# Mean of k's squares from a high and a low fp32r part, with two more rows of q1 in front of it

## The reference, cut to what matters

```python
k = apply_rope(rms_norm(k, k_norm_g[l]), cos, sin)      # mean of squares over the 64 values of a head
q = apply_rope(rms_norm(q, q_norm_g[l]), cos, sin) * q_scale
attn = sliding_sink_attention(q, k, v, sinks[l])
pool = multiscale_pool(u, w_pool[l], pool_scale[l])
h = h + jnp.concatenate([attn, pool], axis=-1) @ w_out[l]
```

## Time and profile before

| what | value |
|---|---|
| median of 3 runs | 1054.25 us (1054.16 to 1055.2) |
| the profiled execution's own time | 1054.56 us |
| its span | 1052.8 us |
| PE busy | 1036.8 us, 98% of the span, 7896 matmuls |
| DVE busy | 687.1 us, 65% |
| ACT busy | 466.1 us, 44% |
| POOL busy | 103.7 us, 10% |
| chain that ended last, by engine | PE 84%, DVE 9%, ACT 4%, issue 2% |
| granted TensorE clock, mean | 0.998 of full speed |

### The profile page before, as it was taken

The page is one execution under the profiler, slowest core; times in us unless marked ns, Lnnn a source line. Parts: engine busy times, 40 slices in busy tenths (PEclk is TensorE's granted clock), DMA queues, the critical chain, the costliest instruction groups (busy, mean ns, idle before and its releaser), DMA issues.

```text
span 1052.8 us, 18748 instructions
## 1 busy us (share of the span) xinstructions
PE 1036.8 (98%) x7896; PEld 990.2 (94%) x7896; DVE 687.1 (65%) x1023; ACT 466.1 (44%) x710; POOL 103.7 (10%) x108
## 2 busy tenths in 40 slices
PE   8999999999999999999999999999999999999998
PEld 7998999999999999999999889999889998899987
DVE  6768645669945599455547784565797557975452
ACT  6986535333423443223338773453442334423322
POOL 1253000110001100011003510000000000000000
PEclk9999999999999999999999999999999999999999
DMA  7210332231333222322231203232223332232212
GB/s 236 87 53 34 106 96 80 81 100 62 117 95 110 81 81 81 121 81 91 84 107 51 81 4 118 81 110 91 81 81 120 99 103 80 80 121 90 92 60 80
DMA packets 94107, 94.96 MB, mean 90 GB/s; under 512 B 3424, under 2 KB 92856, under 8 KB 94024
## 3 DMA queue, kind: packets, MB, share of 16 engines
q1 hardware_dynamic: 93456, 93.58, 27.9%
q10 hardware_dynamic: 312, 0.18, 0.1%
q0 software_dynamic: 256, 0.01, 0.0%
HBM read 91.65 MB, written 2.10 MB: 89 GB/s over the span
## 4 chain that ended last, share of the span: by engine, by line
PE 84%; DVE 9%; ACT 4%; issue 2%; DMA 0%; DVEq 0%; SPq 0%; ACTq 0%
PE slot L571 65%; PE slot L985 12%; PE slot L789 2%; PE slot L629 1%; ACT sumsq L1256 1%; PE slot L1045 1%; PE slot L849 1%; PE slot L856 1%; DVE ms_work L1657 1%; PE slot L821 1%; DVE w_lo L424 1%; DVE k_dup L1669 1%; DVE nmax L1720 1%; DVE m_op_lo L1930 0%; DVE sink_arg L1725 0%
## 5 line engine op out<-in xcount | busy, mean ns | idle before, releaser
L571 PE MATMUL slot<-x_hi,w_hi 128*128 128x264 f32 (+2 forms) x1516 | 353.7, 300 | 0.0
L571 PE MATMUL slot<-x_lo,w_hi 128*128 128x264 f32 (+2 forms) x1516 | 350.0, 298 | 0.0
L571 PE MATMUL slot<-x_hi,w_lo 128*128 128x264 f32 (+2 forms) x1516 | 349.5, 297 | 0.0
L571 PEld LDWEIGHTS slot<-x_hi,w_hi 128*128 128x128 f32 x1516 | 245.8, 189 | 11.1 <-issue 0.7
L571 PEld LDWEIGHTS slot<-x_lo,w_hi 128*128 128x128 f32 x1516 | 244.7, 189 | 7.3
L571 PEld LDWEIGHTS slot<-x_hi,w_lo 128*128 128x128 f32 x1516 | 244.4, 189 | 7.5
L424 DVE TENSOR_TENSOR w_lo<-raw,w_hi 128x2048 fp32r<-128x2048 f32 (+2 forms) x68 | 151.7, 2231 | 99.9 <-ACT w_hi L413 99.9
L413 ACT ACTIVATE w_hi<-raw 128x2048 fp32r<-128x2048 f32 (+2 forms) x68 | 124.0, 1823 | 150.2 <-PE slot L571 95.1
L1149 POOL TENSOR_TENSOR work<-work 128x528 f32<-128x528 f32 (+1 forms) x32 | 42.0, 1312 | 706.4 <-DVE work L1890 348.1
L1435 ACT ACTIVATE work<-gate,par_all 128x528 f32<-128x528 f32 (+1 forms) x44 | 31.9, 730 | 133.2 <-DVE gate L1605 67.4
L985 PE MATMUL slot<-m_op_hi,w_hi 128*128 128x264 f32 (+1 forms) x256 | 73.8, 288 | 1.3 <-DVE h L1966 0.7
(11 more groups left out here) (226 smaller groups left out, 1673.0 us busy)
## 6 DMA issues: line engine op xcount, KB each, us to landing
raw<-in_w_gate SPq DMA_DIRECT2D x44, 512.0 KB, 4.8
raw<-in_w_up SPq DMA_DIRECT2D x44, 512.0 KB, 4.5
raw<-in_w_down SPq DMA_DIRECT2D x32, 512.0 KB, 4.1
raw<-in_w_in SPq DMA_DIRECT2D x19, 512.0 KB, 4.9
raw<-in_w_out SPq DMA_DIRECT2D x16, 512.0 KB, 4.0
raw<-in_w_down SPq DMA_DIRECT2D x16, 384.0 KB, 3.5
x_in<-in_x SPq DMA_DIRECT2D x4, 512.0 KB, 6.7
out<-y_out SPq DMA_DIRECT2D x4, 256.0 KB, 2.4
```

What stands on the lines that cost most here:

```text
L571: ins = nc.tensor.matmul(out_part, w[ws][:, r, cols], a[:, k, tokens], start=first and n == 0 and w is w_hi and a is a_hi, stop=end and w ...
```

## The change

k's squares are no longer multiplied in fp32. ACT copies them to `pool_hi[:, 0]` (fp32r) right behind the square, having waited for the square itself; DVE subtracts that copy from them into `pool_lo[:, 0]`, between `q_tile(0)` and `split_lo(2)`; in layer 0 ACT also copies the matrix to fp32r (`block_r`). PE runs four fp32r matmuls (two parts, two halves) in place of the two fp32 ones. In PE's order two further rows of q1 come in front of the mean, behind the transposes of v; they are the same rows that came behind it before.

```diff
@@ PE @@
-                k_squares = head_sq[:].rearrange("p b q -> p (b q)")[:, 0:L]
-                column_mean("k_sq", l, block_mean, k_squares, headsq_ready, l * 5 + 1)
-                dense(ps.slot("q1"), U_Q % 2, P, eight[ahead:], x_hi, x_lo, first=False, tail=l + 1 == DEPTH).then_inc(filled[ps.slot("q1")], 1)
+                q1_rows = dict(first=False, tail=l + 1 == DEPTH)
+                dense(ps.slot("q1"), U_Q % 2, P, eight[ahead:ahead + 2], x_hi, x_lo, last=False, **q1_rows)
+                s = open_slot("k_sq", l)
+                pe.wait_ge(block_ready, 1)
+                pe.wait_ge(ksqlo_ready, l + 1)
+                for n, part in enumerate((pool_hi, pool_lo)):
+                    for half in range(2):
+                        ins = nc.tensor.matmul(slot[s][:, half, 0:HALF], block_r[:], part[:, 0, half * HALF:(half + 1) * HALF],
+                                               start=n == 0, stop=n == 1)
+                ins.then_inc(filled[s], 1)
+                dense(ps.slot("q1"), U_Q % 2, P, eight[ahead + 2:], x_hi, x_lo, **q1_rows).then_inc(filled[ps.slot("q1")], 1)
@@ ACT @@
                 nc.scalar.activation(head_sq[:].rearrange("p b q -> p (b q)")[:, 0:L], k_dup[:, 0], ACT.Square)\
                   .then_inc(headsq_ready, 1)
+                act.wait_ge(headsq_ready, l * 5 + 1)
+                nc.scalar.activation(pool_hi[:, 0], head_sq[:].rearrange("p b q -> p (b q)")[:, 0:L], ACT.Copy)\
+                  .then_inc(ksqhi_ready, 1)
                 if l == 0:
                     act.wait_ge(prep_ready, 1)
                     act.wait_ge(const_loaded, 16)
+                    nc.scalar.activation(block_r[:], block_mean, ACT.Copy).then_inc(block_ready, 1)
                     nc.scalar.activation(mean_r[:], all_mean, ACT.Copy).then_inc(mean_ready, 1)
@@ DVE @@
                 q_tile(0)
+                dve.wait_ge(ksqhi_ready, l + 1)
+                nc.vector.tensor_tensor(pool_lo[:, 0], head_sq[:].rearrange("p b q -> p (b q)")[:, 0:L],
+                                        pool_hi[:, 0].bitcast(f32), ALU.subtract).then_inc(ksqlo_ready, 1)
                 split_lo(dve, l, 2)
```

More of the change, by code:

```diff
@@ L160, in build_trunk @@
         mean_r = sb(ctx, "mean_r", [P, P], f32r)
+        block_r = sb(ctx, "block_r", [P, P], f32r)
         log_eps = sb(ctx, "log_eps", [P, 1])
@@ L259, in build_trunk @@
         sq_added = sem("sq_added")
+        ksqhi_ready, ksqlo_ready, block_ready = sem("ksqhi_ready"), sem("ksqlo_ready"), sem("block_ready")
         sumhi_ready, sumlo_ready, mean_ready = sem("sumhi_ready"), sem("sumlo_ready"), sem("mean_ready")
```

## The result

| | before | changed |
|---|---|---|
| median, same session | 1054.18 us (14 runs, 1054.03 to 1056.43) | 1056.68 us (14 runs, 1054.95 to 1059.41) |
| ratio | | 1.0022, 95% interval 1.0015 to 1.0029 |
| the profiled execution | 1054.56 us, span 1052.8 | 1058.31 us, span 1056.5 |
| granted TensorE clock of the profiled execution | 0.998 | 0.992 |

The changed kernel is slower by 2.5 us, 0.22%. The forecast was 1055.45 within 1053.4 to 1057.0: the side was right and so was the mechanism that it gave, but half of the size was missing. The profiled execution is one of the slower ones of the changed kernel, so its stages show the effect large.

A forecast was written before the change was run, and what follows sets the result against it. It took the line on ACT and DVE, from v's transposes to m3a, to bound the kernel: PE's -0.82 us lost in waits, the chain's +1.19 paid, so 1054.25 + 1.2 = 1055.45 us, within 1053.4 to 1057.0.

The forecast's parts named there:

- What bounds the stretch: From v's transposes to m3a, ACT and DVE set the time; PE has some 0.8 us to spare in layer 0.
- PE's saving: k's mean on PE: four fp32r matmuls cost 0.49 us instead of 0.90, saving 0.41 a layer, 0.82 in all.
- The cover of the two rows: Two q1 rows before the mean hide the wait for the low part, by 1.5 us (layer 0) and 0.1 (layer 1).
- ACT's delay: Copy, wait for the square and layer 0's `block_r` delay `v_meta` on the chain: +0.50 and +0.69 us, sum +1.19.
- DVE and POOL: Rival: the moved `split_lo(2)`, POOL's cosine product and `sine_part(0)` block each other, adding +1.2 us: 1056.7; chance 0.11.
- the rival's two sums: Layer 1, end of `sine_part(0)`: 563.2 against the reciprocal due at 563.3, or 564.1 with the longest lengths, 0.8 late.
- The sum: Whole kernel: PE's -0.82 disappears in PE's waits, the chain gets +1.19, so median 1054.25 + 1.2 = 1055.45 us, +0.11%.
- the two waits: PE's waits between v's transposes and m3a: 0.2 us for a q tile's squares, 0.6 us at m3a for `pool_lo`.
- The range: Whole run: from PE's gain, 1053.4, to 1057.0, the slower rival with some spread.
- The forecast's own range: Whole run: 1054.8 to 1056.2 us, from the bounds of the chain's terms and 0.5 us of spread between medians.
- What would show it: Signs in the changed profile: four short fp32r records, m3a at about 79.8 and 601.5, `v_meta` at 38.15 in layer 0.
- The grown wait at L697: PE's wait for the q tile's squares grows from 0.2 to over 1 us in layer 0; a like one in layer 1.

The follow-up runs named there:

- PE's part alone: Kernel before, with ACT writing the squares straight to `pool_hi`, PE multiplying `pool_hi` twice in fp32r, copy and subtraction left out: 1054.33 us, ratio 1.0002.
- the delay alone: Changed kernel with PE's old lines back (fp32 mean, no q1 rows in front); ACT's copy, `block_r` and DVE's subtraction stay: 1055.83 us, ratio 1.0011.
- shortening the chain: Changed kernel, DVE remaking the squares instead of ACT's copy, ACT's other copies moved, q1 and POOL reordered: 1052.32 us, ratio 0.9984.
- the idle time filled: Changed kernel plus 9 (layer 0) and 7 (layer 1) unread matmuls before PE's wait for the q2 and q3 squares: 1055.00 us, repeat 1055.54.
- the one with two matmuls: Kernel before plus two unread matmuls, layer 0 only, before PE's wait for the squares of q2 and q3: 1054.17 us, ratio 0.9996.

## Why the prediction was right or wrong, point by point

- **What bounds the stretch.** Right. PE's part alone gave 1.0002, the delay alone 1.0011, and shortening the chain 0.9984.
- **PE's saving, 0.41 us a layer.** Right in size (0.42) and in worth (none).
- **The cover of the two rows.** It held in both layers. But it isn't needed: without the rows PE waits 1.33 us at the mean in layer 1 and the time is 1.5 us better. That nothing follows if the cover fails was right (m3a +0.48 and +0.71, as with the idle time filled); that the cover itself could do harm, by leaving all of the idle time to lie ahead of the q means, was not seen.
- **ACT's delay, 0.50 + 0.69.** Measured +0.49 and +0.68 at `v_meta`, +0.52 and +0.70 at m3a with the idle time filled.
- **DVE and POOL.** The meeting took place and did nothing. The timelines of DVE and POOL in the changed kernel, layer 1:

```profile
560.99 2.29 DVE L426 TENSOR_TENSOR w_lo<-raw,w_hi 128x2048 fp32r<-128x2048 f32 x1
563.45 1.58 DVE L1646 TENSOR_TENSOR v_T<-head,sq 128x528 f32<-128x528 f32 x1 [0.17 <-issue]
565.41 3.45 DVE L1674 RECIPROCAL ms_work<-ms_work 128x528 f32<-128x528 f32 x1 [0.38 <-ACT ms_work L1322]
...
561.76 2.71 POOL L1122 TENSOR_TENSOR rot_c<-head,sq 128x528 f32<-128x528 f32 x1 [13.79 <-ACT sq L1305]
```

  POOL's product took 2.71 us: it began in the middle of the split, which ended at 563.28, and ended 1.2 us later. `sine_part(0)` took 1.58 us and ended 0.56 behind POOL. By the Trainium skill (SBUF — State Buffer, "Who interferes with whom") the one of the two that starts second is blocked for the whole of the first. The trace agrees: what is left behind the first one's end, 1.2 and 0.56 us, is a little less than each takes alone (1.3 and 0.71). The reciprocal was still released by ACT's root, 0.38 us behind `sine_part(0)`. So the first of the rival's two sums, "just in time", is the one that came out.
- **The sum.** Here the prediction fell short: "PE's -0.82 disappears in PE's waits" books the grown waits of an engine with time to spare at nothing. They were not free: behind them the clock was low for 10.2 and 6.9 us in place of 3.4 and none, and PE, with under 1 us to spare in this stretch, came late with the scores, for which DVE then waited. The missing term is 1.68 us between the changed kernel (1056.68) and the same with its idle time filled (1055.00), measured in different sessions, and 1.05 us in the side by side repeat (1056.59 and 1055.54). The trace of before already held the warning, a granted clock of 0.72 from 66 to 72 us, in the stretch where PE had under 1 us to spare; the low stretch began 4.4 us behind the end of PE's wait of 0.20 us. I read the two waits, and only the mean clock of the run.
- **The range.** That 1056.68 lies within 1053.4 to 1057.0 is in part luck. The forecast's own range ended at 1056.2. The wide one reached to 1057.0 because of the rival in which DVE and POOL meet, whose sum of 1056.7 is the measured time; but that meeting cost nothing, and the same number came from the clock, which no rival names.
- **What would show it.** The grown wait at L697 was named as a sign that the forecast was right. It was one, and it was also, by the filled kernel, the cause of most of what the forecast lacked. m3a came at 81.28 and 603.60 where 79.8 and 601.5 were forecast; and since the root of layer 0 lay 0.52 us earlier in this execution, the distance from the root is the fairer measure, +2.54 us where +0.5 was forecast. `v_meta` at 37.64 in place of 38.15 is that same shift.

## What to carry to other kernels

An engine that is busy 98% of the span can still have time to spare where it matters: follow the chain of waits through the stage before booking a saving. And a wait of TensorE is not free just because it lies off the chain: here the clock was at half behind it, and the scores came late. Ask where the idle time will lie, and read the granted clock by windows behind every wait, before and after. A precision split costs its copy and its subtraction on the engines that make it; if one of these is on the chain, look for an engine that is idle at that moment (here DVE, for 1.0 us) or for work that can leave the chain (here two tables).

## What the runs showed of the hardware

- The granted clock fell to half 1.4 to 4.4 us behind the end of idle times of 0.2 to 1.14 us, where small matmuls (2 and 16 columns, among larger ones) followed. In both profiles of the rows behind the mean, an idle time of 1.3 us in layer 1 that was followed by 264- and 258-column matmuls had no low stretch behind it. The Trainium skill (TensorE: Matmul & The Clock Gate, "A second HAM failure mode: psum-queue depth-cycling") tells of another kernel, in bf16, whose short idle times between groups of matmuls made the clock go back and forth between its two levels. The runs here agree in kind: with the waits filled, 4 of 22 executions had a mean clock of 0.996 or less, and 17 of 23 without.
- What decides a single low stretch stays open. Behind the same wait of 1.0 or 1.1 us in layer 0 the kernel with the rows behind the mean had none in one execution and one of 6.8 us in another, and three kernels had some of 3.4 to 6.8 us where no wait of PE is listed ahead (the filled one, the one with two matmuls, the shortened one).
- A low stretch cost only what PE had not to spare: the kernel before had one of 3.4 us in layer 0 and still waited 0.6 us at m3a.
- ACT's wait for its own preceding instruction cost 0.12 us (a start 0.65 behind the square's, against 0.53 to 0.54 without the wait).
